# FFN up products on TensorE: wide and narrow products alternate chunk by chunk

## What is computed

```python
def swiglu(h, w13, w2):
    gate, up = jnp.split(h @ w13, 2, axis=-1)
    return (jax.nn.silu(gate) * up) @ w2

for l in range(2):
    ...
    x = x + 0.5 * swiglu(rms_norm(x, ffn1_norm[l]), ffn1_w13[l], ffn1_w2[l])
    ...                       # a gated linear recurrence (l = 0), a stick-breaking attention (l = 1)
    x = x + 0.5 * swiglu(rms_norm(x, ffn2_norm[l]), ffn2_w13[l], ffn2_w2[l])
```

## Time and profile before

| | |
|---|---|
| median of 3 runs | 1478.03 us (1477.88 to 1478.25) |
| the profiled execution's own time | 1478.09 us |
| its span, first to last instruction | 1476.3 us |
| TensorE (PE) busy | 1463.5 us, 99% |
| weight loads (PEld) busy | 1291.2 us, 87% |
| DVE busy | 1241.4 us, 84% |
| ACT busy | 836.8 us, 57% |
| DMA engines, mean over the span | 211 GB/s |
| granted TensorE clock | 1.00 (2.4 GHz) |

### The profile page before, as it was taken

The page is one execution under the profiler, slowest core; times in us unless marked ns, Lnnn a source line. Parts: engine busy times, 40 slices in busy tenths (PEclk is TensorE's granted clock), DMA queues, the critical chain, the costliest instruction groups (busy, mean ns, idle before and its releaser), DMA issues.

```text
span 1476.3 us, 23180 instructions
## 1 busy us (share of the span) xinstructions
PE 1463.5 (99%) x8772; PEld 1291.2 (87%) x8772; DVE 1241.4 (84%) x1743; ACT 836.8 (57%) x1225; POOL 128.3 (9%) x76
## 2 busy tenths in 40 slices
PE   9999999999999999999999999999999999999999
PEld 8888899988888898888779888887789988999888
DVE  7999998989998869999777988875677898787864
ACT  6554668655456645556785454654665455565452
POOL 0013100001311102111020111100000121000110
PEclk9999999999999999999999999999999999999999
DMA  7667754656675547667233877644235587346660
GB/s 274 255 242 252 274 209 164 228 197 235 243 268 198 228 159 284 246 247 262 86 142 122 304 254 262 246 164 143 82 140 210 196 307 301 127 150 233 245 228 29
DMA packets 44703, 311.41 MB, mean 211 GB/s; under 512 B 5760, under 2 KB 6016, under 8 KB 7488
## 3 DMA queue, kind: packets, MB, share of 16 engines
q1 hardware_dynamic: 42192, 303.33, 56.2%
q0 software_dynamic: 1840, 5.73, 1.3%
q10 hardware_dynamic: 576, 1.05, 0.2%
HBM read 308.98 MB, written 1.05 MB: 210 GB/s over the span
## 4 chain that ended last, share of the span: by engine, by line
PE 86%; DVE 8%; ACT 3%; issue 2%; DMA 1%; SPq 0%; DVEq 0%; ACTq 0%
PE psum L2169 18%; PE psum L2180 10%; PE psum L2204 7%; PE psum L2207 7%; PE psum L2208 7%; PE psum L2070 7%; PE psum L2077 7%; PE psum L2076 7%; DVE w_lo L1182 3%; PE psum L2420 3%; PE psum L2425 3%; PE psum L2426 3%; DVE buf L1191 1%; DVE buf L1405 1%; PE psum L2217 1%
## 5 line engine op out<-in xcount | busy, mean ns | idle before, releaser
L1182 DVE TENSOR_TENSOR w_lo<-raw,w_hi 128x1024 fp32r<-128x1024 f32 x478 | 592.1, 1256 | 68.3 <-ACT w_hi L582 68.1
L582 ACT ACTIVATE w_hi<-raw 128x1024 fp32r<-128x1024 f32 x477 | 484.4, 1048 | 91.0 <-PE psum L2180 35.7
L2169 PE MATMUL psum<-u,w_hi 128*128 128x512 f32 x1376 | 325.9, 389 | 0.0
L2169 PEld LDWEIGHTS psum<-u,w_hi 128*128 128x128 f32 x1376 | 258.3, 188 | 53.6
L2070 PE MATMUL psum<-u,w_hi 128*128 128x256 f32 (+1 forms) x872 | 251.9, 289 | 1.3 <-ACT buf L925 0.9
L2077 PE MATMUL psum<-u,w_lo 128*128 128x256 f32 (+1 forms) x872 | 246.4, 283 | 0.0
L2076 PE MATMUL psum<-u,w_hi 128*128 128x256 f32 (+1 forms) x872 | 246.4, 283 | 0.0
L2204 PE MATMUL psum<-w_hi,hid_hi 128*128 128x512 f32 x528 | 206.8, 392 | 0.3 <-issue 0.2
L2207 PE MATMUL psum<-w_hi,hid_lo 128*128 128x512 f32 x528 | 206.5, 391 | 0.0
L2208 PE MATMUL psum<-w_lo,hid_hi 128*128 128x512 f32 x528 | 205.5, 389 | 0.0
L2180 PEld LDWEIGHTS psum<-u,w_lo 128*128 128x128 f32 x1376 | 176.4, 191 | 6.7
(11 more groups left out here) (324 smaller groups left out, 1738.5 us busy)
## 6 DMA issues: line engine op xcount, KB each, us to landing
raw<-stream SPq DMA_DIRECT2D x287, 1024.0 KB, 4.8
buf<-tab POOLq DMA_DIRECT2D x2, 768.0 KB, 4.9
raw<-stream SPq DMA_DIRECT2D x2, 512.0 KB, 5.7
x<-x_in SPq DMA_DIRECT2D x2, 512.0 KB, 6.3
buf<-stream POOLq DMA_DIRECT2D x1, 1024.0 KB, 5.0
buf<-ctx_in POOLq DMA_DIRECT2D x1, 1024.0 KB, 7.5
buf<-poolmat POOLq DMA_DIRECT2D x1, 1024.0 KB, 5.1
out<-x ACTq DMA_DIRECT2D x4, 256.0 KB, 2.0
```

The lines of the kernel that those rows point to most:

```text
L582: sc.activation(w_hi[:, u], raw[:, u], ACT.Copy).then_inc(S.hi_ready, 1)
L1182: ve.tensor_tensor(w_lo[:, u], raw[:, u], w_hi[:, u].bitcast(F32), ALU.subtract).then_inc(S.lo_ready, 1)
L2169: ins = te.matmul(bank2(bank), w_hi[:, at + k * P:at + (k + 1) * P], both[:, k, :], start=k == 0, stop=False, skip_group_check=True)
```

## The change

`wide_up` calls a new function, `woven`, once for each of the two units. It issues, for each of the eight 128-row chunks, the wide matmul and right behind it the narrow one. Before the unit's first matmul it waits for `lo_ready` of that unit; the waits for `hi_ready` are gone, since `lo_ready` comes after it. Both `unit_used` increments now sit on the first matmul of a unit. The matmuls, their operands and their banks are the same.

```diff
+            def woven(c, i, bank):
+
+                at = (c % RING) * UNIT
+                unit_ready(c, i)
+                for k in range(NC):
+                    w = slice(at + k * P, at + (k + 1) * P)
+                    ins = te.matmul(bank2(bank), w_hi[:, w], u_both[:, k, :], start=k == 0, stop=False, skip_group_check=True)
+                    if k == 0:
+                        first = ins
+                    last = te.matmul(bank2(bank)[:, 1, :], w_lo[:, w], u_hi[:, k, 0:T], start=False, stop=k == NC - 1,
+                                     skip_group_check=True)
+                return first, last
+
             def wide_up(c, i, j, bank, h0, a0):
 
                 if not isinstance(j, int) or j > PLAIN + 1:
                     pe.wait_ge(S.up_added, a0 + j - PLAIN - 1)
                 else:
                     pe.wait_ge(S.up_scaled, h0 + j - 1)
-                wide_hi(c, i, bank).then_inc(S.unit_used, 1)
-                wide_hi(c + 1, i, bank + 1)
-                wide_lo(c, i, bank)
-                first, last = wide_lo(c + 1, i, bank + 1)
-                first.then_inc(S.unit_used, 1)
+                for n in range(2):
+                    first, last = woven(c + n, i, bank + n)
+                    first.then_inc(S.unit_used, 1)
                 last.then_inc(S.up_ready, 1)
                 begun[0] = c + 1
```

## The result

| | before | after |
|---|---|---|
| median | 1478.04 us (1477.88 to 1478.25) | 1486.07 us (1485.67 to 1486.83) |
| the profiled execution's own time | 1478.09 us | 1486.83 us |
| its span | 1476.3 us | 1485.0 us |

The account below looks back on a forecast made before the run. The prediction took PE, busy for 99% of the span and 86% of the chain of waits, as the bound. Its terms, 7.5 + 0.75 - 0.26 = +8.0 us on 1478.09, gave 1486 us, range 1470 to 1491.

Parts of the forecast that it names:

- Part 1, the pairs: FFN wide steps: a wide matmul behind a narrow one costs 0.0065 us more; 0.104 a step, 7.5 us over 72.
- 0.004 and 0.0095: Extra us per wide matmul: 0.004 in six behind a narrow block, 0.0095 for isolated ones in the attention's running sums.
- Part 2, the stall: First wide step of the first FFN: PE waits for DVE's low weights, needed earlier; one stall, +0.75 us.
- Part 3, the wait at 135.20: First FFN: PE's one wait, for DVE's subtraction of the down unit, goes because PE is later by then; -0.26 us.
- Part 4, edits at nothing: Wide steps: two fewer waits a step and the second unit's `unit_used` 1.8 us earlier cost nothing.
- Sum: Whole kernel: 7.5 + 0.75 - 0.26 = +8.0 us on the profiled execution's 1478.09, giving 1486 us.
- The rival "no change": FFN pairs cost 0.346 us in any order; 1477.1 to 1478.6, about 1478 us; chance 0.22.
- The rival "faster": FFN pairs cost 0.340 us, narrow matmuls 0.113 between wide ones; -7 to -7.6, about 1470.5 us; chance 0.18.
- The rival "DVE late often": Wide steps: late low weights stall PE repeatedly; three 0.75 us stalls plus the pairs' cost give 1488 us; chance 0.02.

Follow-up runs that it names:

- eights: Changed kernel's interleaving by groups of eight: 8 wide, 8 narrow, 8 wide, 8 narrow a step; 1480.60 us in one run, 1478.16 before in the same session.
- twos: Changed kernel's interleaving by groups of two wide and two narrow matmuls instead of single ones; 1479.26 us, ratio 1.0006 (0.9996 to 1.0015).
- the one with the waits alone: Kernel before with its matmul order kept and only the low-weight waits moved earlier, as in the changed kernel; 1479.94 us, ratio 1.0009 (1.0000 to 1.0019).
- a group of four: Changed kernel's interleaving by groups of four wide and four narrow matmuls instead of single ones; 1483.30 us in one run.

## Why the prediction was right, point by point

- *Part 1, the pairs, 0.104 us a step, 7.5 in all.* Measured 0.10 a step, in FFNs and, where tried, in MLPs: 72 x 0.10 = 7.2. The neighbours seen in the attention's sums carried over. The size of 0.0065 was luck in part. It was put on the wide matmul alone, as the middle of 0.004 and 0.0095, with the narrow one left at its ordinary cost. Measured, a wide one pays 0.009, which is the upper of the two values, and a narrow one gives 0.003 back; only their sum, 0.0067 a pair, is what was forecast. The two values were also not bounds of one effect: the experiments show that the cost depends on how many of each length stand together, with 0.02 a step for eights and under 0.01 for twos.
- *Part 2, the stall, 0.75 us.* Found where it was expected, for L1182, and nowhere else in the wide steps; 0.90, and 0.08 more for the slow matmul behind it. Of the 0.90, 0.75 lasts until DVE's end at 40.10. The working left out the 0.15 from there to the matmul's start at 40.25, and the slow first matmul (0.47 long instead of 0.39). ACT's copy was to move by 0.25; it moved from 44.50 to 46.17, which is 0.66 more than the 1.01 of the whole trace, since both the stall and the block ahead of it were longer than the working had them. It did no harm, since PE was late by more.
- *Part 3, the wait at 135.20, -0.26.* Gone, in the changed kernel and in the one with the waits alone. It was worth 0.33: the row's 0.26 is the idle time of the weight loads, and the step with the wait took 8.62 instead of 8.29.
- *Part 4, edits at nothing.* The waits at the hand-over between units cost nothing that shows.
- *Sum.* +8.0 forecast; 8.03 by the medians. In the profiled execution 8.7, of which 1.0 is ahead of the change. The three terms measure 7.2 + 0.98 - 0.33 = 7.9, 0.2 more than the 7.7 that is left; 0.13 of it goes between the third and the fourth FFN, where nothing was changed.
- *The rival "no change".* It falls with the 0.353 of a pair. The Trainium skill (TensorE: Matmul & The Clock Gate, section Back-to-back issue gap) calls its columns / 2.4 plus 2.5 ns the gap of an isolated matmul, and says that in a stream of loads and matmuls both set the spacing; "whatever stands beside it" is the prediction's own reading of the formula. In this trace a stream of equal lengths is slower than that formula: 0.2267 for 512 columns is 213 ns and 13 more. Beside another length it costs more still.
- *The rival "faster".* Its mechanism was half there: a narrow matmul between wide ones costs 0.11 to 0.12. What it missed is that the wide one pays 0.23 to 0.24, and with 320 columns in the narrow matmul the wide one pays still. Its 0.113 came from one stretch; the other stretch of the same calls shows 0.117, with which the gain of a pair is half as large.
- *The rival "DVE late often".* One wait in the trace, the one priced.

**Open.** Why unequal lengths cost, and why by groups of one, two, four and eight so differently. Ruled out by runs: the bank, the alternation of the weight tiles, the waits, and the load behind the narrow matmul as the only cause. What a load reads changes the pace, as the kernels with one broadcast column show, but no run tells whether it is the excess or the ordinary cost that they lower.

## What to carry to other kernels

On an engine that is busy for 99% of the span, the cost of a matmul is the distance to the next start, and it is worth looking up in the trace for each pair of neighbours: durations and busy shares don't tell it. A stretch of six matmuls elsewhere in the same kernel gave the sign of 7 us here and, with luck, their size. Keep matmuls of one length together when both kinds are otherwise free to move; singly alternating lengths was the worst grouping of those tried. An order that needs an operand earlier costs only where the margin is gone, and it can take back a wait that was there before.

## What the runs showed that I had not expected

- The cost is not monotone in the number of changes: one change from wide to narrow a step (before) costs 8.29 us a step, two (by unit) 8.31, four 8.35 (5.59 + 2.77, rounded), eight (twos) 8.29 to 8.30, sixteen (singles) 8.39.
- The neighbours act across functions: the twelve down products take 2.73 us behind a pair of narrow ones, 2.75 behind a long block or singles and 2.77 behind a group of four, though nothing in them changes.
- A 256-column matmul can cost 0.113, 0.115 or 0.120 us. In `pool_shift`, where the stationary operand is one column broadcast to 128 (it is not the moving operand of 256 columns that is broadcast), it costs 0.113 in one stretch and 0.117 in the other. In groups of two between wide ones it costs 0.115 on average. With a broadcast low column between wide ones, it costs 0.118 to 0.119.
- The kernel's time moves by about 1 us between executions through the first 9 us alone (the first product starts at 8.82 before and at 9.83 in the profile after), which is larger than several of the effects here. Only the trace, step by step, tells them.
